# A two-layer decoder with routed experts: the expert choice split by chunk, the router's neighbours on TensorE reordered, counts and gates moved behind the first list round

## The reference

```
def moe_ffn(x, w_router, router_bias, w_gate, w_up, w_down, ws_gate, ws_up, ws_down):
    scores = jax.nn.sigmoid((xf @ w_router).astype(jnp.float32))
    sel_scores = scores + router_bias.astype(jnp.float32)
    grp = sel_scores.reshape(-1, N_GROUPS, N_EXPERTS // N_GROUPS)
    grp_score = lax.top_k(grp, 2)[0].sum(-1)
    _, top_grp = lax.top_k(grp_score, TOP_GROUPS)
    ...
    _, top_idx = lax.top_k(jnp.where(expert_mask, sel_scores, -jnp.inf), TOP_K)
    gates = jnp.take_along_axis(scores, top_idx, axis=-1)
    gates = gates / gates.sum(-1, keepdims=True) * ROUTE_SCALE
    routed = routed_experts(xf, top_idx, gates, w_gate, w_up, w_down)
    shared = (jax.nn.silu(xf @ ws_gate) * (xf @ ws_up)) @ ws_down
    return (routed + shared).reshape(b, t, d)
```

## Time and profile before

| | |
|---|---|
| median of 3 runs | 1407.73 us (1406.64 to 1408.94) |
| the profiled execution | 1404.73 us |
| its span | 1402.9 us |
| PE busy | 1348.4 us, 96% |
| DVE, ACT, POOL busy | 429.9, 220.2, 348.8 us |
| bytes moved by DMA | 475.60 MB, mean 339 GB/s |
| routing in layer 0, layer 1 | from about 180 and 875 us |
| expert rounds | from about 217.6 and 910 us |

### The profile page before, as it was taken

How to read it: one execution, slowest core, us unless ns; L and a number is a source line. 1 busy time by engine, 2 the same in 40 slices (tenths; PEclk the granted TensorE clock), 3 DMA queues, 4 the chain that set the end, 5 groups by cost and what they waited for, 6 DMA issues and landing times.

```text
span 1402.9 us, 20390 instructions
## 1 busy us (share of the span) xinstructions
PE 1348.4 (96%) x7932; PEld 701.5 (50%) x7932; DVE 429.9 (31%) x1277; ACT 220.2 (16%) x546; POOL 348.8 (25%) x369
## 2 busy tenths in 40 slices
PE   8999999999999999999989999899999999999897
PEld 4755454454454454454447554454545555444443
DVE  0442563222222222222154424523232222222223
ACT  1154120101101101101021541111111111011010
POOL 2031435222222222232000213442323232222200
PEclk9999999999999999999999999999999999999999
DMA  9832378999999999999975234799999999999993
GB/s 328 318 119 78 135 251 330 420 415 417 419 418 416 418 420 420 418 418 418 350 254 200 92 114 155 255 406 418 418 416 419 418 419 415 420 419 418 418 420 139
DMA packets 108194, 475.60 MB, mean 339 GB/s; under 512 B 16260, under 2 KB 22712, under 8 KB 75232
## 3 DMA queue, kind: packets, MB, share of 16 engines
q1 hardware_dynamic: 92960, 442.73, 78.3%
q0 software_dynamic: 15168, 32.01, 6.3%
HBM read 491.21 MB, written 3.75 MB: 353 GB/s over the span
## 4 chain that ended last, share of the span: by engine, by line
PE 76%; DMA 16%; DVE 3%; issue 1%; POOL 1%; ACT 1%; SPq 1%; POOLq 0%; DVEq 0%; ACTq 0%
PE bank L636 25%; PE bank L666 13%; PE bank L615 13%; DMA ring<-in_w_up_dram 9%; DMA arena<-in_w_up_dram 6%; PE bank L714 6%; PE bank L725 5%; PE bank L941 3%; PE bank L836 1%; PE bank L611 1%; PE bank L654 1%; PE bank L984 1%; PE bank L817 1%; PE bank L717 1%; PE bank L588 1%
## 5 line engine op out<-in xcount | busy, mean ns | idle before, releaser
L1875 POOL DMA_INDIRECT arena<-h_rows,rank_i x256 | 255.6, 998 | 648.4 <-DVE arena L1543 503.8
L636 PE MATMUL bank<-ring,arena 128*64 128x256 f32 x2816 | 313.8, 380 | 15.0 <-DMA ring<-in_w_up_dram 10.9
L636 PEld LDWEIGHTS bank<-ring,arena 128*64 128x64 f32 x2816 | 204.1, 137 | 136.5 <-issue 27.3
L615 PE MATMUL bank<-arena 128*128 128x512 f32 x512 | 247.1, 606 | 1.4 <-ACT arena L1157 1.4
L1576 DVE TENSOR_TENSOR arena<-arena,bank 128x256 f32<-128x256 f32 x64 | 26.9, 421 | 567.7 <-ACT arena L1152 567.6
L666 PE MATMUL bank<-ring,arena 128*64 128x512 f32 x704 | 160.8, 599 | 0.0
L1538 DVE STREAM_TRANSPOSE arena<-arena 128x256 f32<-128x256 f32 x256 | 141.5, 610 | 29.3 <-DMA arena<-h_rows,rank_i 25.8
L636 PE MATMUL bank<-arena 128*64 128x256 f32 x1280 | 142.7, 380 | 6.5 <-DMA arena<-in_w_up_dram 6.5
L1157 ACT ACTIVATE arena<-bank 128x512 f32<-128x512 f32 x128 | 76.4, 597 | 436.8 <-PE bank L666 436.8
L615 PEld LDWEIGHTS bank<-arena 128*128 128x128 f32 x512 | 87.2, 190 | 89.1 <-issue 86.0
L636 PEld LDWEIGHTS bank<-arena 128*64 128x64 f32 x1280 | 91.5, 137 | 62.7 <-issue 10.3
(11 more groups left out here) (210 smaller groups left out, 897.9 us busy)
## 6 DMA issues: line engine op xcount, KB each, us to landing
ring<-in_w_gate_dram SPq DMA_DIRECT2D x44, 2048.0 KB, 27.1
ring<-in_w_up_dram SPq DMA_DIRECT2D x44, 2048.0 KB, 27.9
ring<-in_w_down_dram SPq DMA_DIRECT2D x44, 2048.0 KB, 27.1
arena<-in_w_gate_dram SPq DMA_DIRECT2D x20, 2048.0 KB, 27.3
arena<-in_w_up_dram SPq DMA_DIRECT2D x20, 2048.0 KB, 29.4
arena<-in_w_down_dram SPq DMA_DIRECT2D x20, 2048.0 KB, 27.3
ring<-in_w_in_dram SPq DMA_DIRECT2D x8, 2048.0 KB, 22.5
ring<-in_w_o_dram SPq DMA_DIRECT2D x4, 2048.0 KB, 12.3
```

Of the source, the lines that this page charges most:

```text
L615: last = mm(bank[SUM_BANKS[n][half]][0:w, :], selg[:, u, t0:t0 + w], y_sb[:, u, half * 512:(half + 1) * 512], start=False, stop=stop, skip ...
L636: last = mm(bank[5][64 * e:64 * e + 64, part * F:(part + 1) * F], xgT[:, u, kk, 64 * e:64 * e + 64], w[:, e, kk, :], start=(kk == 0), stop ...
L1875: pool.indirect_dma_start(out=xg[:, u, b, :], out_offset=None, in_=h_rows, in_offset=bass.IndirectOffsetOnAxis(ap=rank_i[:, at:at + 1], ax ...
```

## The change

The choice of the experts becomes a function, `choose_experts(ns)`. It is called first for all chunks but 2, as soon as their scores and the rows of chunk 1 are ready, then for chunk 2 alone; the same operations as before work on fewer columns in each call, and `chosen_ready` is raised twice per layer. On ScalarE, `router_rows` of the first part goes ahead of the normalisation of chunk 2 and `scores` of the first part ahead of its features. On TensorE the first score transposition goes ahead of `turn_h` of chunk 2, single and half pieces of `shared(1)` stand around the router, `chosen_turned` is raised behind the transpositions, the counts come later with a semaphore of their own (`chosen_counted`), and `turn_lists` stands ahead of the last two pieces of `shared(2)` and of `open_sums`. The order of the shared products becomes 1, 0, 2 in layer 0. On VectorE the reciprocal and the gates (`close_gates`) go behind the first of the eight list rounds. On SP the load of slot 7 waits for `shared(2)`, the counts and the gathers of pair 0; the load of slot 8 behind it keeps its other two waits. The diff, with the parts left out that only rename `SHARED` to `HIDDEN` where the hidden rows are counted, and the unchanged body of the choice:

```diff
@@ -107,7 +107,8 @@
 SUM_BANKS = [(4,), (0, 1), (2, 3)]
 EXTRA_SUMS = [EXTRA * len(row) for row in SUM_ORDER]
 SCORED = [3, 5]
-SHARED = tally([[1, 2] + ([0] if l == 0 else []) for l in range(DEPTH)])
+SHARED_ORDER, HIDDEN_ORDER = [[1, 0, 2], [1, 2]], [[1, 2, 0], [1, 2]]
+SHARED, HIDDEN = tally(SHARED_ORDER), tally(HIDDEN_ORDER)
 
 RET_ORDER = [[1, 2, 0], [1, 2]]
 RET = tally(RET_ORDER)
...
@@ -529,13 +531,13 @@
                     t0, w = CHUNKS[n]
                     sp.dma_start(h_quads[t0:t0 + w, :, QUARTER:ROW], gates[0:w, n, :].unsqueeze(1).to_broadcast([w, 4, E]))\
                         .then_inc(gates_stored, 16)
-                sp.wait_ge(shared_done, SHARED[l][0 if l == 0 else 2])
-                sp.wait_ge(chosen_turned, l + 1)
+                sp.wait_ge(shared_done, SHARED[l][2])
+                sp.wait_ge(chosen_counted, l + 1)
                 sp.wait_ge(gates_stored, (48, 80)[l])
+                sp.wait_ge(gathered[0][l], 64)
                 load_part(l, 2, 2, 1)
                 sp.wait_ge(sums_open, l + 1)
                 sp.wait_ge(h_stored, (48, 80)[l])
-                sp.wait_ge(gathered[0][l], 64)
                 load_part(l, 2, 2, 2)
                 hold_here(sp, count_ready, l + 1)
                 most = sp.value_load(count_i[0:1, 0:1], min_val=0, max_val=T)
...
-                def shared(n, k0=0, k1=KC):
+                def shared(n, k0=0, k1=KC, cols=slice(0, 2 * F)):
 
                     t0, w = CHUNKS[n]
                     for kk in range(k0, k1):
                         if n:
-                            last = mm(bank[7 - n][0:w, :], hT[:, kk, t0:t0 + w], wsgu[:, kk, :], start=(kk == 0), stop=(kk == KC - 1))
+                            last = mm(bank[7 - n][0:w, cols], hT[:, kk, t0:t0 + w], wsgu[:, kk, cols], start=(kk == 0), stop=(kk == KC - 1))
...
@@ -1002,30 +1004,39 @@
                 features_ready((l, 0), 1)
                 router(lo, 144)
                 pe.wait_ge(ws_gate_up_in, l * 32 + 32)
-                shared(1, 0, 2)
+                shared(1, 0, 1)
+                turn_scores(QUERIES[l][:-1], 0)
                 turn_h((l, 0), 2)
-                turn_scores(QUERIES[l][:-1], 0)
-                shared(1, 2, 4)
+                shared(1, 1, 2)
                 features_ready((l, 0), 2)
                 router(144, T)
-                shared(1, 4, 5)
+                shared(1, 2, 3, slice(0, F))
                 turn_scores([2], 1)
-                shared(1, 5, KC)
-                shared(2, 0, 5)
+                shared(1, 2, 3, slice(F, 2 * F))
+                shared(1, 3, KC - l)
 
                 pe.wait_ge(const_in, 16)
-                pe.wait_ge(chosen_ready, l + 1)
+                pe.wait_ge(chosen_ready, l * 2 + 2)
                 ch = rows3["chosen"]
                 for n in QUERIES[l]:
                     t0, w = CHUNKS[n]
-                    pe.transpose(bank[4][0:64, t0:t0 + w], ch[0:w, n, :], ident[0:w, 0:w])
+                    last = pe.transpose(bank[4][0:64, t0:t0 + w], ch[0:w, n, :], ident[0:w, 0:w])
+                last.then_inc(chosen_turned, 1)
+                if l == 0:
+                    shared(0)
+                else:
+                    shared(1, KC - 1, KC)
+                pe.wait_ge(left_ready, l + 1)
                 for n in QUERIES[l]:
                     last = mm(bank[4][:, 448:512], k["ones"][0:CHUNKS[n][1], :], ch[0:CHUNKS[n][1], n, :],
                               start=(n == QUERIES[l][0]), stop=(n == 2))
-                last.then_inc(chosen_turned, 1)
-                shared(2, 5, KC)
+                last.then_inc(chosen_counted, 1)
+                shared(2, 0, 6)
+                pe.wait_ge(score_ready, SCORED[l])
                 if l == 0:
-                    shared(0)
+                    pe.wait_ge(shared_sig, SHARED[l][0])
+                turn_lists(l, 0)
+                shared(2, 6, KC)
...
@@ -1060,10 +1071,6 @@
                 last = open_sums(2)
                 if l:
                     last.then_inc(sums_open, 1)
-                pe.wait_ge(score_ready, SCORED[l])
-                if l == 0:
-                    pe.wait_ge(shared_sig, SHARED[l][0])
-                turn_lists(l, 0)
                 turn_hidden(1)
                 turn_hidden(2)
...
@@ -1136,6 +1143,8 @@
                     if j and order[j - 1]:
                         rows_to_features((l, ph), order[j - 1])
                     if ph == 0:
+                        if n == order[-1]:
+                            ahead()
                         normalise(l, ph, n)
                 if between:
                     between()
@@ -1296,8 +1305,7 @@
                         w = CHUNKS[n][1]
                         act.activation(rows3["score"][0:w, n, :], bank[7][0:w, n * E:(n + 1) * E], ACT.Sigmoid).then_inc(score_ready, 1)
 
-                layer_norm(l, 0, lambda: router_rows(lo, 144, 0))
-                scores(QUERIES[l][:-1], 0)
+                layer_norm(l, 0, lambda: router_rows(lo, 144, 0), lambda: scores(QUERIES[l][:-1], 0))
                 router_rows(144, T, 1)
                 scores([2], 1)
                 act.wait_ge(const_in, 16)
...
-                shared_gate(1)
-                shared_gate(2)
-                if l == 0:
-                    shared_gate(0)
-                for n in SHARED[l]:
+                for n in SHARED_ORDER[l]:
+                    shared_gate(n)
+                for n in HIDDEN_ORDER[l]:
                     hidden_features(n)
                 hold_here(act, count_ready, l + 1)
...
@@ -1503,10 +1509,12 @@
                     dve.match_replace(left, eight, left, 0.0).then_inc(list_step[l], 1)
                     hold_here(dve, list_step[l], r * (CAP // 4) + 2 * j + 2)
 
-            def first_lists(l):
+            def first_lists(l, between):
 
                 left = mo["left"][0:64, FIRST[l]:T]
                 for j in range(CAP // 8):
+                    if j == 1:
+                        between()
                     eight = mo["list"][0:64, 8 * j:8 * j + 8]
                     dve.max(eight, left).then_inc(list_step[l], 1)
                     dve.wait_ge(list_step[l], 2 * j + 1)
...
@@ -1727,59 +1735,72 @@
+                def choose_experts(ns):
+
+                    nq, own_chunks = len(ns), slice(ns[0], ns[-1] + 1)
+                    part = {n: s3[n][:, own_chunks, :] for n in s3}
+                    cubes = {n: cube[n][:, own_chunks, :, :] for n in cube}
+                    step(dve.tensor_tensor(part["biased"], part["score"], rbias[:, :].unsqueeze(1).to_broadcast([128, nq, E]), ALU.add))
+                    after_steps()
...
+                    for n in ns:
+                        step(dve.max(best8[:, :], s3["biased"][:, n, :]))
+                        after_steps()
+                        step(dve.match_replace(s3["picked"][:, n, :], best8[:, :], s3["biased"][:, n, :], TAKEN))
+                        after_steps()
+                    dve.tensor_scalar(part["chosen"], part["picked"], -2e38, None, ALU.is_le).then_inc(chosen_ready, 1)
+
+                dve.wait_ge(small_moe, l * 32 + 32)
+                dve.wait_ge(h_ready_tok, NORM[(l, 0)][1])
+                dve.wait_ge(score_ready, SCORED[l] - 1)
+                choose_experts(QUERIES[l][:-1])
+                dve.wait_ge(h_ready_tok, NORM[(l, 0)][2])
+                dve.wait_ge(score_ready, SCORED[l])
+                choose_experts([2])
+
                 own_chunks = slice(QUERIES[l][0], 3)
                 nq = len(QUERIES[l])
                 part = {n: s3[n][:, own_chunks, :] for n in s3}
-                cubes = {n: cube[n][:, own_chunks, :, :] for n in cube}
-                dve.wait_ge(h_ready_tok, NORM[(l, 0)][2])
...
-                dve.tensor_scalar(part["chosen"], part["picked"], -2e38, None, ALU.is_le).then_inc(chosen_ready, 1)
-                dve.wait_ge(chosen_ready, l + 1)
+                gsum, ginv = mo["gsum"][:, own_chunks], mo["ginv"][:, own_chunks]
+                dve.wait_ge(chosen_ready, l * 2 + 2)
                 step(dve.tensor_tensor(part["tmp"], part["score"], part["chosen"], ALU.mult))
                 after_steps()
-                gsum, ginv = mo["gsum"][:, own_chunks], mo["ginv"][:, own_chunks]
                 step(dve.tensor_reduce(gsum, part["tmp"], AX, ALU.add))
-                after_steps()
-                step(dve.reciprocal(ginv, gsum))
-                after_steps()
-                dve.scalar_tensor_tensor(gates[:, own_chunks, :], part["tmp"], ROUTE_SCALE,
-                                         ginv.unsqueeze(2).to_broadcast([128, nq, E]), ALU.mult, ALU.mult)\
-                    .then_inc(gates_ready, 1)
+
+                def close_gates():
+                    after_steps()
+                    step(dve.reciprocal(ginv, gsum))
+                    after_steps()
+                    dve.scalar_tensor_tensor(gates[:, own_chunks, :], part["tmp"], ROUTE_SCALE,
```

(20 more changed lines are left out.)

60 lines of the change are left out of this document (29 added, 31 removed).

## The result

The changed kernel takes 1410.46 us (median of 20 runs, 1406.59 to 1413.49) against 1406.31 (20 runs, 1403.48 to 1410.53) for the kernel before, run beside it: ratio 1.0025, 95% interval 1.0017 to 1.0033. It is slower: by 3.5 us by the ratio, by 4.2 us by the two medians. The profiled execution took 1408.56 us, its span is 1406.7, 3.8 more than before.

The account below looks back on a forecast made before the run. The unbroken stream of weight transfers was taken to bound both expert rounds: 5.0 us longer per layer, 3.7 and 3.1 earlier, so +3.2 on a median of 1407.73, giving 1410.9 us. Range 1406.5 to 1414.

Parts of the forecast that it names:

- the gain of the chain: Routing to the first stream transfer: the stream begins 3.7 us earlier in layer 0 and 3.1 in layer 1.
- The stream and slot 7: Weight loads of both expert rounds: slot 7's 2.097 MB join the unbroken stream, 5.0 us per layer (4.7 to 5.4).
- a share under 1 behind 214: DMA windows of the changed profile: shares under 1 behind 214 us would show the forecast wrong.
- The choice: VectorE: two chunks chosen early in 5.21 us, chunk 2 alone in 3.58; choice ends at 192.6 instead of 194.79 in layer 0.
- From `left` to the gathers: Left 3.0 and 3.57 us earlier, less 0.6 and 0.5 for the gates: gathers 2.4 and 3.1 earlier (layers 0, 1).
- The start in layer 0: Stream start in layer 0: 1.3 us earlier because slot 7, unlike slot 8, does not wait for open_sums(0).
- TensorE behind the lists: 5.3 us of matmuls added between lists and pair 0; pair 0 starts about 216.1, at no cost to the end.
- The sum: Whole kernel: +1.3 us in layer 0, +1.9 in layer 1, nothing between the layers; together +3.2, 1410.9.
- The chain's gain reaches the end: Rival, first pair of each round: TensorE, not the stream, sets the end; -4.6 us, 1403.1; chance 0.12.
- the choice is not earlier: Rival, VectorE's choice (also called the lost choice): the chain gains nothing; +8.7 us, 1416.4; chance 0.05.
- The two nearly cancel: Rival, both layers: transfers cost 4.7, the chain gains most; +0.2 and +0.9 us, 1408.8; chance 0.33.
- TensorE uses up its slack: Rival, work behind the lists: low clock makes open_sums(0) and slot 8 late, stream hole of 1 us; +4.2, 1411.9; chance 0.1.

Follow-up runs that it names:

- a_fill: Changed kernel with all of shared(2) ahead of turn_lists, slot 7 still waiting for pair 0's gathers: 1410.41 us, ratio 1.0029.
- a_dvefin: Changed kernel with the scale and shift of chunk 2's rows moved from GpSimd to VectorE: 1407.04 us, ratio 1.0015.
- b_wait7: Kernel before with only SP's wait for pair 0's gathers moved ahead of slot 7: 1413.53 us, ratio 1.0013; timed again (_2) 1414.71, 1.0058.
- a_pool_late: Changed kernel with GpSimd's scale and shift of chunk 2's rows held until left is ready: 1424.44 us, ratio 1.0097.
- set C: Third set of experiments, on a chip of its own; the kernel before beside them took 1406.43 us.
- a_fill7_2: Changed kernel, all of shared(2) ahead of turn_lists, slot 7 not waiting for the gathers, second timing: 1405.70 us, ratio 0.9998; first timing (a_fill7) 1412.31, 1.0013.
- before again: The kernel before, unchanged, timed and profiled once more: 1407.8 us, ratio 1.001.
- set A: First set of experiments, on a chip of its own; the kernel before beside them took 1411.75 us.
- again: The changed kernel, unchanged, timed and profiled once more: 1410.52 us, ratio 1.0033 to the kernel before.
- a_free7_2: Changed kernel with the wait for the gathers put back behind slot 7's load, second timing: 1409.61 us, ratio 1.0024; first timing (a_free7) 1413.71, 1.0011.
- a_dvefin_fill7: Changed kernel with the edits of a_fill7_2 and a_dvefin together: 1403.66 us, ratio 0.9983 to the kernel before.
- sets B and C: Second and third sets of experiments, each on its own chip; the kernel before took 1406.14 and 1406.43 us there.

## Why the prediction was right, and which term was not

The sign and the cause were right: slot 7's bytes in the full stream cost more than the earlier lists give back. The time, 1410.46 against 1410.9, is closer than the working deserves. The base was 1.4 too high (1407.73 from three runs; twenty gave 1406.31), the rise 1.0 too low (3.2; 4.15 by the medians), and inside the rise the gain of the chain was put at nearly twice its size (3.7 + 3.1, measured 1.9 + 1.8), which an earlier R0 hid. That is luck. Point by point:

**The stream and slot 7: right.** Forecast 5.0 us per layer (4.7 to 5.4). Measured 5.1 and 4.6 in the changed profile; from 4.0 to 5.1 over all pairs of a profile of before with one of a kernel that has slot 7 in the stream (the changed kernel, `a_fill`, `a_dvefin`, `b_wait7`, `a_pool_late`). The lone move cost 8.3 in set C; its price was put at 8.7, the same sum as the rival of the lost choice. The forecast's own sign of being wrong, a share under 1 behind 214, shows only in the run-up to 216; there is no hole behind it.

**The choice: mis-sized.** The forecast had chunk 2's choice end 10.2 us after R0 (192.6 - 182.4) and `left` begin 11.0 after it. They came 11.8 and 12.8 after. The failing term is "5.21 for two chunks": its first addition took 2.17 instead of 0.28 us, because it was moved into the time in which GpSimd works on chunk 2. I had read the 4.2 us of idle VectorE as free and had not looked at what GpSimd did in it. In layer 1 `left` came 10.8 after R1 instead of 12.95, 2.15 earlier, not 3.57. That 192.43 on the clock looks like the forecast's 192.6 is chance: R0 was 1.8 early.

The Trainium skill has the rule: SBUF — State Buffer, SBUF: two separate sides, says that a VectorE instruction with two SBUF inputs and a GpSimd one that reads SBUF exclude each other for the whole of an instruction. The runs agree: 2.17 and 2.10 beside GpSimd, 0.28 without.

**From `left` to the gathers: right in kind.** Of the 1.3 us by which `left` comes earlier in layer 0, 0.65 reach the gathers (32.88 to 32.23 after R0), the gates having been put at 0.6. In layer 1 1.8 of 2.15 arrive. Forecast were 2.4 and 3.1.

**The start in layer 0: right in kind, its size from one execution.** Slot 7 not waiting for `open_sums(0)` was to give 1.3; `b_wait7` and `b_wait7_2` have S0-R0 at 32.79 and 32.89 instead of 34.14 and 33.13, 0.2 to 1.35 less, and `a_fill7_2` shows the wait itself. The 1.3 was what the one profile had; in before again slot 8 was issued 0.3 behind the landed gathers.

**TensorE behind the lists: harmless, as said, in other detail.** Pair 0 began at 215.19 (forecast 216.1), 34.6 after R0 (33.7). The low clock behind the lists is gone, as TensorE is full at 203 to 208. It fell elsewhere: TensorE waited 2.78 us for the choice, and 64 small matmuls then took 3.21 us, with a granted clock of 0.50 at 193 to 195; in `a_fill7`, where the wait was 0.20, they took 1.94.
```profile
192.58 0.77 PE L1023 MATMUL bank<-const,arena 16*64 16x16 f32 x3 [2.78 <-DVE arena L1778]
193.27 3.21 PE L989 MATMUL bank<-arena 128*16 128x128 f32 x64
```
In `a_fill` this stretch too ran at full speed, and its stream is no shorter. The waits for weights grew by 2.2 in layer 0 instead of 3, and the last up tile landed at 1381.8 (forecast "near 1381").

**The sum: right partly by offset.** By its own steps the change costs 3.2 + 2.8 = 6.0 in the profiles, not 3.2: of the forecast 3.7 and 3.1 by which the streams would begin earlier, 1.9 and 1.8 came. Measured is 3.8 in the spans of the two profiles, 3.5 by the ratio, 4.15 by the medians. The 2.2 us between 6.0 and 3.8 are the earlier R0 (1.8) and the shorter R1-P0 (0.5, scatter). R0 lay at 182.4 to 184.8 in the four profiles of kernels in the old order (before twice, `b_wait7` twice) and at 180.2 to 184.3 in the ten of kernels made from the changed one, seven of them below 181.7; the difference is there by 78 us, before any edited line runs. It is mostly TensorE's clock. The same 16 matmuls, before and changed:
```profile
73.67 4.44 PE L799 MATMUL bank<-arena 64*128 64x272 f32 x16
73.12 3.30 PE L801 MATMUL bank<-arena 64*128 64x272 f32 x16
```
Before, the granted clock is 0.64 at 74 to 76 and 0.51 at 76 to 78; in the changed profile it is 1.00. In all four profiles of the old order it fell there; of the ten others it fell in five and not in the five with R0 at 180.2 to 180.6. What makes it fall there, and if the new program makes it rarer, stays open. The medians speak for the program. By the sums of R0 to P0 and R1 to P1, `b_wait7_2` costs 8.5 us over before (the mean of its two profiles) and measured 8.3. The seven kernels of the new order that were timed outside set A should cost 6.3 (changed), 6.0 (again), 6.0 (`a_free7_2`), 7.1 (`a_fill`), 0.0 (`a_fill7_2`), 4.4 (`a_dvefin`) and 0.0 (`a_dvefin_fill7`). They measured 4.2, 4.4, 3.2, 4.3, -0.7, 0.9 and -2.8, each 0.7 to 3.5 less. This suggests, from one profile each, that some 2 us of what the new order gives lie outside the stretches that the prediction reasoned on. It had them at nothing ("Everything between the layers hangs rigidly on the last pairs"; R1-P0 was 198.2 to 202.0 over the profiles).

**Rivals.** "The chain's gain reaches the end" and "the choice is not earlier" fell by the table. "The two nearly cancel" needed a chain that gains 3.2 and 3.8; it gained 1.9 and 1.8, and its +1.1 lies under the measured interval (2.4 to 4.6 us). "TensorE uses up its slack" fell by `a_fill`, where the low clock and the late `open_sums(0)` were there and no hole came. TensorE's pauses in pair 0 in set A, a cause that neither the prediction nor its rivals had, went with a price of slot 7 of 1.8 us there instead of 8.3. What makes them isn't known; the profile names no semaphore.

## What to carry to other kernels

When the DMA engines are full from one point to the end of a stage, as here, a load moved from an idle gap into that stretch costs about its bytes over the rate: 2.1 MB cost 4.0 to 5.1 us here, more than the 1.8 us or so by which the same edit brought the stretch forward. An engine's idle time is free only against what its neighbours do in it: look at GpSimd before moving VectorE work with two SBUF inputs. And take the spans apart at the same events in both kernels, since a mis-sized term and a shift elsewhere can add up to a right total.

## What was not expected of the hardware

- VectorE's 128 x 128 addition took 2.17 us beside a GpSimd addition over 128 x 1024 and 0.28 without it.
- In set A TensorE stopped within pair 0, for no semaphore, in both layers of `b_wait7` and `a_fill7` (in layer 0 1.5 and 2.1 us by the brackets); the 64 matmuls took 9.3 and 14.8 us, the latter in part at the lower clock. In no profile of sets B and C did it, and there they took 7.13, or 8.6 to 8.8 at a clock partly low (`a_free7_2`). `a_free7` and `a_pool_late`, also of set A, show no such stop. Before measured 1411.75 on the chip of set A, 1406.14 and 1406.43 on the others.
- VectorE did GpSimd's product and sum over 128 x 1024 in 1.23 and 1.22 us, GpSimd took 2.00 and 2.34.
- The granted clock fell near 74 us in nine of fourteen profiles, in one and the same stretch of code; the 16 matmuls there took 4.2 to 4.5 us instead of 3.30, and R0, 100 us later, came at 181.6 to 184.8 instead of 180.2 to 180.6.
